# Adding the last layer's result to the output by accumulating DMA transfers

## The reference

```
for l in range(DEPTH):                       # DEPTH = 2
    ...
    xp = xp + gate_p * rms_norm(op, g_post[l])
    xs = xs + gate_s * rms_norm(os_, g_post[l])
return (xp, xs, ...)                          # y_prompt, y_sample
```

## Time and profile before

| what | value |
|---|---|
| median of 3 runs | 2036.15 us (2035.3 to 2037.24) |
| the profiled execution's own time | 2035.46 us |
| its span in the trace | 2033.8 us |
| TensorE busy | 1954.1 us, 96% of the span |
| VectorE busy | 1424.5 us, 70% |
| GpSimd busy | 180.8 us, 9% |
| DMA | 386.69 MB, mean 190 GB/s |

### The profile page before, as it was taken

How to read it: one execution, slowest core, us unless ns; L and a number is a source line. 1 busy time by engine, 2 the same in 40 slices (tenths; PEclk the granted TensorE clock), 3 DMA queues, 4 the chain that set the end, 5 groups by cost and what they waited for, 6 DMA issues and landing times.

```text
span 2033.8 us, 42282 instructions
## 1 busy us (share of the span) xinstructions
PE 1954.1 (96%) x16148; PEld 1843.3 (91%) x16148; DVE 1424.5 (70%) x2084; ACT 846.3 (42%) x1307; POOL 180.8 (9%) x127
## 2 busy tenths in 40 slices
PE   4999999999999999999999999997999999999995
PEld 3889999999999999999999999997888887789995
DVE  5597777777777777797778986666433456669777
ACT  3243333333333333454555643344443444445443
POOL 1200000000000000000000240002222122201002
PEclk9999999999999999999999999998999999999997
DMA  9966555565655555744464334447313249852447
GB/s 392 404 234 226 205 192 191 191 201 202 208 203 203 201 194 194 251 148 156 138 251 148 135 104 149 159 150 271 93 65 93 83 134 345 258 176 96 138 155 271
DMA packets 134902, 386.69 MB, mean 190 GB/s; under 512 B 13906, under 2 KB 44498, under 8 KB 131858
## 3 DMA queue, kind: packets, MB, share of 16 engines
q1 hardware_dynamic: 129682, 368.52, 51.9%
q0 software_dynamic: 5120, 16.78, 2.6%
HBM read 353.92 MB, written 31.33 MB: 189 GB/s over the span
## 4 chain that ended last, share of the span: by engine, by line
PE 85%; DMA 6%; DVE 5%; ACT 2%; issue 1%; SPq 1%; ACTq 0%; DVEq 0%
PE ps L938 37%; PE ps L942 18%; DMA s<-adastream 4%; PE ps L892 3%; PE ps L1398 3%; PE ps L826 3%; PE ps L1249 2%; PE ps L1424 2%; PE ps L1264 2%; PE ps L1282 2%; PE ps L1339 2%; DMA w_raw<-wstream 1%; PE ps L878 1%; PE ps L833 1%; PE ps L1327 1%
## 5 line engine op out<-in xcount | busy, mean ns | idle before, releaser
L1544 ACT ACTIVATE w_split<-w_raw 128x1024 fp32r<-128x1024 f32 x204 | 215.9, 1058 | 377.8 <-PE ps L942 208.2
L2082 DVE TENSOR_TENSOR w_split<-w_raw,w_split 128x1024 fp32r<-128x1024 f32 x209 | 255.7, 1224 | 139.8 <-ACT w_split L1544 135.1
L938 PE MATMUL ps<-operand_hi,w_split 128*128 128x288 f32 x1224 | 328.5, 295 | 0.0
L938 PE MATMUL ps<-operand_lo,w_split 128*128 128x288 f32 x1224 | 328.3, 294 | 0.0
L769 POOL TENSOR_TENSOR w_split<-w_raw,w_split 128x1024 fp32r<-128x1024 f32 x50 | 134.8, 2696 | 1562.9 <-ACT w_split L1482 1562.9
L938 PE MATMUL ps<-t_hi,w_split 128*128 128x288 f32 x960 | 262.9, 300 | 0.6 <-DVE c_u L2232 0.6
L938 PE MATMUL ps<-t_lo,w_split 128*128 128x288 f32 x960 | 258.0, 295 | 0.0
L938 PEld LDWEIGHTS ps<-operand_hi,w_split 128*128 128x128 f32 x1224 | 229.8, 188 | 0.0
L938 PEld LDWEIGHTS ps<-operand_lo,w_split 128*128 128x128 f32 x1224 | 229.7, 188 | 0.0
L938 PEld LDWEIGHTS ps<-t_hi,w_split 128*128 128x128 f32 x960 | 180.3, 188 | 10.0 <-issue 8.7
L942 PE MATMUL ps<-operand_hi,w_split 128*128 128x288 f32 x1224 | 186.9, 295 | 1.1 <-DVE w_split L2082 1.1
(11 more groups left out here) (397 smaller groups left out, 3911.4 us busy)
## 6 DMA issues: line engine op xcount, KB each, us to landing
w_raw<-wstream SPq DMA_DIRECT2D x169, 512.0 KB, 3.8
ada_ring<-adastream SPq DMA_DIRECT2D x112, 512.0 KB, 4.9
a<-wstream SPq DMA_DIRECT2D x88, 512.0 KB, 4.7
s<-wstream SPq DMA_DIRECT2D x44, 512.0 KB, 3.3
ada_first_ring<-adastream SPq DMA_DIRECT2D x32, 512.0 KB, 9.6
ada_third<-adastream SPq DMA_DIRECT2D x32, 512.0 KB, 6.4
tiles<-y_park SPq DMA_DIRECT2D x12, 1152.0 KB, 7.6
x_residual<-x_in SPq DMA_DIRECT2D x8, 1152.0 KB, 8.7
```

Source lines behind the costliest of these rows:

```text
L938: pe.matmul(PS[:, bank, 0:HALF], WH[:, c.slot, k * P:(k + 1) * P], x(k), start=(first and k == 0 and x is hi), stop=False, skip_group_chec ...
L1544: act.activation(WH[:, c.slot, :], raw, ACT.Copy).then_inc(w_hi_ready, 1)
L2082: dve.tensor_tensor(WL[:, c.slot, :], raw, WH[:, c.slot, :].bitcast(F32), ALU.subtract).then_inc(w_lo_ready, 1)
```

## The change

Neither `X1_ODD` nor `X1_EVEN` is loaded. VectorE multiplies each of the 16 tiles in place in SBUF (tiles 12 to 15 into `B1`) and makes no sum. GpSimd makes no sum either: when tile t is multiplied, it starts a transfer of that tile to its place in `y_out` with an accumulating add, so that the DMA engines add it to the x1 that lies there. SP issues no store in the tail and only waits for the ends.

```
+        def last_scaled(t):
+            return YA[:, (t - 8) * T:(t - 7) * T] if 8 <= t < 11 else YM[:, :] if t == 11 else B1[:, t * T:(t + 1) * T]
 SP:
-            for g, idx in enumerate((1, 2)):
-                sp.wait_ge(w_used, pair_operand(1, PAIRS - 1, idx).at(1))
-                sp.dma_start(X1_ODD[:, 4 * g:4 * g + 4, :], tile_pairs(y_out)[:, 4 * g:4 * g + 4, 1, :]).then_inc(x_landed[g], 16)
-            def x1_even(g, landed):
-                sp.dma_start(X1_EVEN[:, 4 * g:4 * g + 4, :], tile_pairs(y_out)[:, 4 * g:4 * g + 4, 0, :]).then_inc(landed, 16)
             sp.wait_ge(w_used, pair_operand(1, PAIRS - 1, 4).at(1))
             b1_back(0, 4)
-            x1_even(0, x_landed[3])
             b1_back(4, 8)
-            sp.wait_ge(x_landed[2], 112)
-            sp.wait_ge(w_used, pair_operand(1, PAIRS - 1, 6).at(1))
-            x1_even(1, x_landed[2])
-            for n in range(KT // 2):
-                c, d = slice(2 * n * T, (2 * n + 1) * T), slice((2 * n + 1) * T, (2 * n + 2) * T)
-                sp.wait_ge(y_added, n + 1)
-                sp.dma_start(y_out[:, c], X1_EVEN[:, n, :]).then_inc(stored, 16)
-                sp.wait_ge(yout_ready, n + 1)
-                sp.dma_start(y_out[:, d], X1_ODD[:, n, :]).then_inc(stored, 16)
             sp.wait_ge(ckv_stored, 16)
-            sp.wait_ge(stored, 16 * (2 + KT))
+            sp.wait_ge(y_added, 16 * KT)
+            sp.wait_ge(stored, 16 * 2)
 GpSimd:
-            for n in range(KT // 2):
...
-                pool.wait_ge(out_normed, 2 * n + 1)
-                pool.tensor_tensor(X1_EVEN[:, n, :], X1_EVEN[:, n, :], B1[:, c], ALU.add).then_inc(y_added, 1)
+            for t in range(KT):
+                pool.wait_ge(out_normed, t + 1)
+                pool.dma_start(y_out[:, t * T:(t + 1) * T], last_scaled(t), accum_op=ALU.add).then_inc(y_added, 16)
 VectorE:
-            def add(t):
...
             for t in range(KT):
-                tile = B1[:, t * T:(t + 1) * T]
-                out = odd_bank(t) if t % 2 else halves(tile)
-                if t % 2 and t >= 7:
-                    dve.wait_ge(yout_ready, t // 2 - 2)
+                out = halves(last_scaled(t))
                 if t < 12:
                     if t % 4 == 0:
-                        dve.wait_ge(x_landed[t // 4], 112)
-                    tile = tile if t < 8 else YA[:, (t - 8) * T:(t - 7) * T] if t < 11 else YM[:, :]
-                    last = dve.tensor_tensor(out, halves(tile), PS[:, 6:8, 0:HALF], ALU.mult)
+                        dve.wait_ge(x_landed[t // 4], 96 if t < 8 else 112)
+                    last = dve.tensor_tensor(out, out, PS[:, 6:8, 0:HALF], ALU.mult)
...
                 last.then_inc(out_normed, 1)
-                if t >= 2 and t % 2 == 0:
-                    add(t - 1)
-            add(KT - 1)
```

More of the change, by code:

```diff
@@ L797, in _ @@
             rest(Chunk(W_OUT + 3))
-            for n in range(KT // 2):
-                c = slice(2 * n * T, (2 * n + 1) * T)
-                if n % 4 == 0:
-                    pool.wait_ge(*((x_landed[2], 128) if n else (x_landed[3], 80)))
-                pool.wait_ge(out_normed, 2 * n + 1)
-                pool.tensor_tensor(X1_EVEN[:, n, :], X1_EVEN[:, n, :], B1[:, c], ALU.add).then_inc(y_added, 1)
+            for t in range(KT):
+                pool.wait_ge(out_normed, t + 1)
+                pool.dma_start(y_out[:, t * T:(t + 1) * T], last_scaled(t), accum_op=ALU.add).then_inc(y_added, 16)
         @block.tensor
@@ L2809, in _ @@
                 dve.wait_ge(wo["scaled"][j], KT // 2)
-            def odd_bank(t):
-                b = 2 * (t // 2 % 3)
-                return PS[:, b:b + 2, 0:HALF]
-            def add(t):
-                dve.wait_ge(out_normed, t + 1)
-                x = halves(X1_ODD[:, t // 2, :])
-                dve.tensor_tensor(x, x, odd_bank(t), ALU.add).then_inc(yout_ready, 1)
             for t in range(KT):
-                tile = B1[:, t * T:(t + 1) * T]
-                out = odd_bank(t) if t % 2 else halves(tile)
-                if t % 2 and t >= 7:
-                    dve.wait_ge(yout_ready, t // 2 - 2)
+                out = halves(last_scaled(t))
                 if t < 12:
                     if t % 4 == 0:
-                        dve.wait_ge(x_landed[t // 4], 112)
-                    tile = tile if t < 8 else YA[:, (t - 8) * T:(t - 7) * T] if t < 11 else YM[:, :]
-                    last = dve.tensor_tensor(out, halves(tile), PS[:, 6:8, 0:HALF], ALU.mult)
+                        dve.wait_ge(x_landed[t // 4], 96 if t < 8 else 112)
+                    last = dve.tensor_tensor(out, out, PS[:, 6:8, 0:HALF], ALU.mult)
                 else:
```

## The result

The change made the kernel slower: 2046.95 us (median of 5, 2046.19 to 2050.54) against 2035.85, a ratio of 1.0057 with a 95% interval of 1.0045 to 1.0069. That is 11.1 us, where 9.5 were forecast (a time of 2045.6).

The account below looks back on a forecast made before the run. TensorE is busy for 96% of the span, but the tail from 2012.52 is VectorE's; first tile at 2013.27, plus 2.4 fixed, 24.9 of transfers, 2.7 closing and 2.35 added gave 2045.6 us, range 2032.5 to 2060.

Parts of the forecast that it names:

- Part 1: VectorE's tail: eight additions go, 5.3 us; the multiplications take 11.0 us, so the last tile is ready at 2023.6.
- Part 2: Before the tail: four loads of x1 leave SP's queue, hidden under TensorE's last pair; worth 0 us.
- Part 3: DMA engines in the tail: the old row is read there too, 1.55 us a tile, 24.9 us for 16.
- the likeliest case: Tail transfers: two packets a row, old row and write, 1.55 us a tile; time 2045.6 us, chance 0.43.
- Part 4: GpSimd issues the tail's transfers in place of SP: 2.4 us fixed latency, issues 0.7 us apart, hidden behind the transfers.
- The fixed part: Latency of a GpSimd transfer beyond its transfer time: 2.4 us taken from its page loads, 1.3 the lower end.
- The sum: First tile at 2013.27, fixed latency 2.4, sixteen transfers 24.9, then 2.7: span 2043.3; with 2.35 added, 2045.6 us.
- the closing: After the last store lands: 2.7 us to the end of the span in which nothing works, unchanged by the change.
- the outer end: Tail transfers: none overlaps the next, each costing 2.4 us and 1.55 us, 63 us in all; time 2084.
- the slower rival: Tail transfers: the add waits for the old row or three movements count; 37.3 us for 16, time 2058.0, chance 0.22.
- GpSimd's pitch: GpSimd in the tail: accumulation is cheap but one transfer starts every 1.24 us; time 2040.1, chance 0.18.
- The other side: Tail transfers: an accumulating row costs no more than a stored one, 0.78 us a tile; time 2033.1, chance 0.17.

## Why the prediction was right

**Part 1, the additions.** The estimate was 11.0 us of VectorE, and 11.0 were measured. The gain was lost behind the DMA engines, as said.

**Part 2, the reload.** Worth nothing: 32.5 us of tail with it, 32.4 without. The reason given was not whole. The last load isn't hidden under TensorE to its end: 0.92 MB of it move in the first 2.3 us of the tail of the kernel before. They cost nothing because the first accumulating packets start only 2.5 us behind the first multiplication.

**Part 3, the add in the transfer.** This is the step that decides, and the likeliest case was the right one: a second read in the tail through engines that were 83% busy. The size was a little low: the stream took 25.7 us for 24.9, 1.61 us a tile for 1.55 (the packet times add up to 27.3, or 2.2 stored tiles of 0.78). The excess lies in its slow beginning: at the 196 GB/s of the full stretch sixteen tiles would take 24.1 us. The rule of the Trainium skill ("Collectives: The Full Stack", section "The bandwidth ceiling: the fold count and why AG ≠ RS ≠ AR") gave 23.9 us by its ratio of 1.93; the trace agrees, with a ratio of 1.97 between the two full stretches (387 and 196 GB/s). The reason from the rows, that the bytes of the hidden load move into the tail, named the right sum. Accumulating into SBUF costs the same, so it isn't the way to DRAM; that it is the second read and not the adding isn't shown.

**Part 4, GpSimd's queue.** The pitch stayed below a transfer's price: 0.54 us for a plain issue, 0.84 to 0.92 for an accumulating one without a backlog. The fixed part of 2.4 us was right: the first packets start 1.8 us after the first multiplied tile (2017.28), and SP's wait ends 0.6 us after the last data.

**The sum.** 0.75 + 2.4 + 24.9 + 2.7 = 30.8 us of tail were forecast and 32.4 measured: 0.76 + 2.4 + 25.7 + 3.5. The 1.6 us are 0.8 of the stream and 0.8 of the closing. Two smaller slips: the 2.35 us added to every span are the median less the span of one execution, whose own time is 1.66 us above its span (1.64 in the changed kernel); and the outer end of the slower rival, 2084, counts the fixed part once too often (63 us behind 2013.27 give about 2081).

**What was wrong in it.** "From there to the end of the span are 2.7 us in which nothing works, and the change leaves them." The 2.7 us were GpSimd's drain, which runs from its last work and not from the last landing; in the changed kernel it ends 3.3 us behind the last landing. The prediction also called GpSimd's additions worth nothing because they were off VectorE's chain. The last of them was on the path that set the end, by way of the drain: moving it gave 1.6 us. Here the error was small by luck: GpSimd's drain again set the end, now behind its own transfers, and the closing came out 0.8 us longer than assumed.

**The rivals.** The slower one (three packets' time a row, 2058) would have needed 2.33 us a tile. GpSimd's pitch was none: half as many accumulations at an unhurried pace still cost 1.67 us each. The other side, an accumulated row at a stored one's price, was wrong by the same numbers; what it would have brought was measured with plain transfers: 2034.2 us for the 2033.1 worked out.

## What to carry to other kernels

An add that a transfer makes isn't free: here it doubled the time that the DMA engines needed for a store. If the reload that it replaces was hidden and the store isn't, the change moves bytes from where they cost nothing to where they cost all; count the tail's DMA time first, and accumulate only as many tiles as that leaves room for. And look at what each engine does at the very end of its program before calling the close of a span fixed: the engine that worked last isn't always the one that is waited for.

## What the runs showed of the hardware

- By packet times an accumulating transfer of 288 KB took the 16 DMA engines 1.67 to 1.70 us, a plain store 0.78 (SP) or 0.81 (GpSimd); 1.56 in rows of twice the length. With full engines the accumulating stream moved 196 GB/s and SP's plain stores 387.
- The stream of accumulations began slowly: 153 GB/s in its first 5 us. No run here shows why.
- The profile's bytes don't count the second source. DRAM reads are 349.20 MB with the add and also with plain transfers in its place, though the sum can't be made without the old rows.
- GpSimd's closing drain ended 5.3 to 5.7 us behind its last sum (before, with tile 14 moved, with SP's plain stores, and with two to four tiles accumulated), and 3.0 to 3.3 us behind the last landing where its own transfers came last.
